# Another order for the sample rows' attention in a two-layer decoder step: page scores first, root transposes among the last keys, the block mask added by GpSimd

## The chip, the cores and the metric

The kernel runs on one core of one Trainium2 chip. The metric is the time of one execution on the device, in microseconds, and lower is better. The core has five engines with queues of their own: TensorE (PE; its weight loads stand as PEld), VectorE (DVE), ScalarE (ACT), GpSimd (POOL) and SyncE (SP, which here only starts transfers). Each engine works through its instructions in the order in which they are written, and waits at semaphores for the others.

## The reference, cut to what matters

One step of a decoder with two layers. 256 prompt rows and 8 x 4 sample rows go through the same weights. The second layer's mixer is sparse attention. The change lies in the part of it for the sample rows: for each of 8 sequences, 4 new rows with 16 heads look at 1024 past keys (16 blocks of 64, of which one in the middle is dropped: top 16 of 17), at the last 512 keys of a window, and at compressed keys.

```python
kb = to_blocks(rmsnorm(sel_full[:, :, 0], kn_g))            # 1024 past keys in blocks of 64, and the new ones
o_sel = selected_branch(q, kb, vb, idx, valid, q_pos, table)
...
    logits = jnp.einsum('btgpd,bngd->...', qg, kg) * SCALE  # sel and window branch alike
    p = masked_softmax(logits + bias, mask, axis=-1)        # the mask holds the unselected blocks
    o = jnp.einsum('...', p, v)
o = gates[:, :, 0] * o_cmp + gates[:, :, 1] * o_sel + gates[:, :, 2] * o_win
return o.reshape(B, T, C_HEADS * HEAD_DIM) @ w_out, ...
```

## The kernel before, in words

The whole step is one program. Activations lie transposed (features on partitions, 256 + 32 rows along the free axis), and each projection goes over units of 256 weight columns: SyncE loads a unit, ScalarE rounds it to its upper part (`wH`), VectorE forms the rest (`wL`), and TensorE multiplies both with the upper and lower part of the activations (`hH`, `hL`). Some 90% of the run is such units.

The sample attention stands between the prompt rows' attention and the output projection (`out_stage`), and nothing else runs on TensorE in that time. The 8 sequences go in 4 pairs, i = 0 to 3. For a pair, 128 partitions hold 2 sequences x 4 groups x 4 rows x 4 heads, and the tile `S` holds their scores: columns 0 to 1023 the pages (selected keys), 1024 to 1055 new keys, 1056 to 1567 the window (local keys), 1568 to 1599 new keys again. The steps of one pair, and who does them:

- **Keys.** The pair's keys come in three sets, c = 0 and 1 (pages) and c = 2 (window). For each set TensorE makes 16 transposes in four lots (`turn_keys`, L2218), into PSUM banks 4 and 5 in turn; ScalarE copies each lot to `KT` (`take_keys`, L1013); TensorE then scores the set into bank c (`score_keys`, L2230). Because there are two banks, lot m + 2 waits for the copy of lot m (`s_taken`). The same two banks serve all other transposes, and `turn_slot` gives each its place in the turn.
- **Norms of the keys.** ScalarE squares six pieces of 1024 (`square_keys`, L1025) into two buffers, VectorE sums each (`sum_squares_of`, L1644); piece n waits for the sum of piece n - 2. Then `variance` (VectorE, L1650), `roots` (ScalarE: a table load, the square root, a table load back, L1036 and L1037), `invert_roots` (VectorE, L1657), `turn_roots` (TensorE, L2239), `take_roots` (ScalarE, L1031), and `spread_roots` (TensorE, L2258), three times four matmuls that spread the factors over the key columns.
- **Softmax.** ScalarE copies the page scores from PSUM to `S` (`keep_scores`, L1046), VectorE the window scores (L1680). VectorE multiplies each of three sets by its factors (`normalise`, L1665), adds the bias (window L1688, pages L1698), adds the mask of the dropped block to the pages (L1702), and takes maxima (window L1691 and L1694, pages L1703 and L1704). ScalarE takes the exponentials (`exps_of`, L1052).
- **Weighing.** TensorE transposes the weights in four lots (`turn_weights`, L2269 and L2272: k = 0 window, 1 and 2 pages, 3 new keys), ScalarE copies them (`take_weights`, L1059 and L1061), TensorE multiplies with the values (`weigh_pages`, L2287, `weigh_new`, L2296). VectorE combines the branches (`gather`, L1718 to L1720), TensorE transposes the result (`turn_output`, L2315), VectorE places it in `zT` (`place_output`, L1730).

Pair i's softmax runs beside pair i + 1's keys; the order in which the pieces of the two stand in each engine's queue is written out by hand at the end of each engine's part. The keys and values of a sequence come by nine transfers for keys and nine for values (`sequence`, L454 to L457), issued by SyncE (even sequences) and GpSimd (odd ones), the keys for pair i + 2 once pair i's are used up, the values once pair i's weighing is over (`s_pv`). After pair 3, ScalarE splits two units of the output weights (`split_out`, L1066), then makes `hH` from `zT` in two halves over all 288 rows (L1113), VectorE makes the two units' `wL` (`lower_out`, L1737) and then `hL` in two halves (L1760), and TensorE begins the output projection (L1834).

Of the kernel before, what the change touches and what calls it, by code (L numbers as in the profile page):

```python
# [122 lines left out]
def emit(nc, a, out):  # L123

    with ExitStack() as ctx:
# [78 lines left out]
        kvs = sb("kvs", [NS, 12 * P], where=spot)  # L204
        KC = sb("KC", [P, NB, 2, 64], where=spot)
# [76 lines left out]
        assert spot[0] <= raw_at  # L282
        spot = [base + 12 * T * 4]
# [66 lines left out]
        bt_summed, bt_act, bt_dve = sem("bt_summed"), sem("bt_act"), sem("bt_dve")  # L350

# [77 lines left out]
        def turn_slot(kind, i, k=0):  # L429

            if i == 0 and kind in ("keys", "roots"):
                return k if kind == "keys" else 13
            if kind == "compressed":
                return 12
            if kind == "weights":
                at_ = (4, 9, 10, 11)[k]
            else:
                i, at_ = i - 1, 16 if kind == "roots" else k + (0, 1, 4)[k // 4]
            return 14 + 17 * i + (at_ if i < 3 else k)

        MULT = (1, 2, 0)
# [142 lines left out]
        def _(pool):  # L584
# [10 lines left out]
            def odd():  # L595
# [89 lines left out]
                for kv in range(2):  # L685
                    sequence(pool, 3, kv)
# [67 lines left out]
        def _(act):  # L754
# [115 lines left out]
            def odd():  # L870
# [134 lines left out]

                def take_keys(i, c):

                    for j in range(4):
                        m = turn_slot("keys", i, 4 * c + j)
                        act.wait_ge(s_turned, m + 1)  # L1010
                        if j == 0 and 3 * i + c >= 2:
                            act.wait_ge(s_scored, 3 * i + c - 1)
                        nc.scalar.activation(KT[(3 * i + c) % 2][:, j, :], ps[:, 4 + m % 2, :], ACT.Copy).then_inc(s_taken, 1)  # L1013
# [25 lines left out]
                def keep_scores(i):  # L1039

                    act.wait_ge(s_scored, 3 * i + 2)
                    if i > 0:
                        act.wait_ge(s_turned, turn_slot("weights", i - 1, 3) + 1)
                    else:
                        act.wait_ge(s_summed, 6)
                    nc.scalar.activation(S[:, 0:PAST], ps[:, 0:2, :].rearrange("p b n -> p (b n)"), ACT.Copy).then_inc(s_kept, 1)  # L1046

                def exps_of(i, k):

                    c0, c1 = ((1056, 1600), (0, 1056))[k]  # L1050
                    act.wait_ge(s_max, 2 * i + k + 1)
# [27 lines left out]
                roots(0)  # L1079
# [3 lines left out]
                nc.scalar.activation(PTc[:, :, :], ps[0:NCMP_S, 4 + m % 2, :].rearrange("p (i q) -> p i q", i=4), ACT.Copy).then_inc(s_taken, 1)  # L1083
                take_roots(0)
                keep_scores(0)
                for i in range(4):
                    if i < 3:
                        square_keys(i + 1, 0)
                        square_keys(i + 1, 1)
                        take_keys(i + 1, 0)  # L1090
                    exps_of(i, 0)
                    if i < 3:
                        square_keys(i + 1, 2)
                        square_keys(i + 1, 3)
                    take_weights(i, 0)
                    if i < 3:
                        take_keys(i + 1, 1)
                    exps_of(i, 1)
                    if i < 3:
                        square_keys(i + 1, 4)  # L1100
                        square_keys(i + 1, 5)
                    for k in range(1, 4):
                        take_weights(i, k)
                    if i < 3:
                        roots(i + 1)
                        take_keys(i + 1, 2)
                        keep_scores(i + 1)
                        take_roots(i + 1)
# [3 lines left out]
                for h in range(2):  # L1112
                    nc.scalar.activation(hH[:, 4 * h:4 * h + 4, :], zT[:, 4 * h:4 * h + 4, :], ACT.Copy).then_inc(ohi_done, 1)  # L1113
# [42 lines left out]
        def _(dve):  # L1156
# [228 lines left out]
            def odd():  # L1385
# [201 lines left out]
                def compressed_branch():  # L1587
# [27 lines left out]
                    sum_squares_of(0, 2)  # L1615
                    sum_squares_of(0, 3)
# [12 lines left out]
                    sum_squares_of(0, 4)  # L1629
                    sum_squares_of(0, 5)  # L1630
# [27 lines left out]

                def normalise(i, c):
# [13 lines left out]
                def softmax(i):  # L1673
# [5 lines left out]
                    dve.wait_ge(s_scored, 3 * i + 3)  # L1679
                    kept = mark(nc.vector.tensor_copy(S[:, 1056:1568], ps[:, 2, :]))  # L1680
                    new_keys(i, 0)
                    new_keys(i, 1)
                    dve.wait_ge(own, kept)
                    normalise(i, 2)
                    if i < 3:
                        sum_squares_of(i + 1, 0)
                    dve.wait_ge(s_mult, 3 * i + 1)
                    biased_ = mark(nc.vector.tensor_tensor(S[:, 1056:1568], S[:, 1056:1568], biasw[:, :], ALU.add))  # L1688
                    normalise(i, 0)
                    dve.wait_ge(own, biased_)  # L1690
# [781 lines left out]
```

## Time and profile before

| | us |
|---|---|
| median of 3 runs | 1770.28 (1765.61 to 1770.8) |
| the profiled execution | 1766.63 |
| its span, first to last instruction | 1764.9 |
| sample attention, TensorE's first score (1372.1) to the first matmul of the output projection (1497.4) | 125.3 |
| mean granted TensorE clock, share of full speed | 0.944 |

TensorE is busy 1591.1 us of the span (90%), VectorE 823.3 (47%), ScalarE 701.9 (40%) and GpSimd 201.7 (11%). A line of a timeline gives the start, how long the piece lasted (several like instructions may be merged, and xN is then their count), the engine, the line of the kernel, the operation with what it wrote and read, and in brackets how long the engine had been idle and what ended that. TensorE's matmuls are written x8 where the program has four: an fp32 product is made in two passes.

### The profile page before, as it was taken

To read this page: it belongs to the slowest core of one execution; us is meant where nothing else is said; L and a number is where in the kernel's file an instruction comes from. 1 tells how busy PE (TensorE), PEld (TensorE's weight loads), DVE (VectorE), ACT (ScalarE), POOL (GpSimd) and SP (SyncE) were. 2 spreads that over 40 slices of the span, in tenths; PEclk is the share of its full clock that TensorE was granted. 3 is DMA by queue.
4 is the path that set the end of the run, shared out by engine and by line. 5 is a ranking of instruction groups with operands and counts; after the bars stand their busy time and mean duration, and the time that the engine had idled before them with its cause. 6 is when DMAs were issued, how large, how long until landed. Compare 5 with 4: busy or idle time off the path is not lost.

```text
span 1764.9 us, 31479 instructions
## 1 busy us (share of the span) xinstructions
PE 1591.1 (90%) x11896; PEld 1438.8 (82%) x11896; DVE 823.3 (47%) x1191; ACT 701.9 (40%) x866; POOL 201.7 (11%) x323
## 2 busy tenths in 40 slices
PE   4799999898789999889999799899988675899997
PEld 2499998796789998779999698888866453899996
DVE  0344443677354443354444432344337765544442
ACT  1333333441343333243333323466446774333332
POOL 6000000193020000000000000222230330000000
PEclk9699999999889999989999789899989998999999
DMA  9667668542167668756755453243562563255442
GB/s 266 212 225 227 223 225 267 168 143 85 50 207 226 224 219 264 231 191 214 222 177 166 151 166 95 79 111 100 181 224 88 158 199 113 72 167 166 154 161 93
DMA packets 269003, 304.77 MB, mean 173 GB/s; under 512 B 9945, under 2 KB 257857, under 8 KB 268792
## 3 DMA queue, kind: packets, MB, share of 16 engines
q1 hardware_dynamic: 260304, 274.96, 49.2%
q0 software_dynamic: 8624, 28.77, 4.9%
q8 instruction: 51, 0.84, 0.2%
q14 instruction: 24, 0.20, 0.0%
HBM read 300.51 MB, written 11.92 MB: 177 GB/s over the span
## 4 chain that ended last, share of the span: by engine, by line
PE 77%; DVE 9%; DMA 7%; ACT 5%; issue 2%; SPq 0%; DVEq 0%; POOL 0%; ACTq 0%; POOLq 0%
PE ps L1834 12%; PE ps L1835 11%; PE ps L1838 11%; PE ps L2050 7%; PE ps L1816 7%; PE ps L1817 6%; PE ps L1818 6%; PE ps L1848 4%; DMA raw<-in_ffn_w_dram 3%; DMA ada<-in_ada_w_dram 2%; PE ps L2034 2%; PE ps L1863 1%; ACT wH L759 1%; DVE wL L1182 1%; PE ps L2147 1%
## 5 line engine op out<-in xcount | busy, mean ns | idle before, releaser
L1182 DVE TENSOR_TENSOR wL<-raw,wH 128x2048 fp32r<-128x2048 f32 (+2 forms) x176 | 365.7, 2078 | 423.1 <-ACT wH L759 423.0
L759 ACT ACTIVATE wH<-raw 128x2048 fp32r<-128x2048 f32 (+2 forms) x176 | 306.1, 1739 | 631.2 <-PE ps L1838 297.1
L1834 PE MATMUL ps<-hL,wH 128*128 128x288 f32 x1008 | 278.9, 304 | 17.1 <-DVE hL L1376 9.2
L1835 PE MATMUL ps<-hH,wH 128*128 128x288 f32 x1008 | 274.2, 298 | 0.0
L1816 PE MATMUL ps<-hH,wL 128*128 128x288 f32 x816 | 250.3, 307 | 12.7 <-DVE hL L1239 12.7
L1818 PE MATMUL ps<-hH,wH 128*128 128x288 f32 x816 | 246.2, 302 | 0.0
L1817 PE MATMUL ps<-hL,wH 128*128 128x288 f32 x816 | 246.1, 302 | 0.0
L1834 PEld LDWEIGHTS ps<-hL,wH 128*128 128x128 f32 x1008 | 192.0, 191 | 31.7 <-issue 13.6
L1834 PE MATMUL ps<-hidL,wH 128*128 128x288 f32 x704 | 194.4, 303 | 0.9 <-ACT wH L759 0.9
L1835 PEld LDWEIGHTS ps<-hH,wH 128*128 128x128 f32 x1008 | 191.9, 190 | 0.2
L1835 PE MATMUL ps<-hidH,wH 128*128 128x288 f32 x704 | 190.1, 296 | 0.0
L1816 PEld LDWEIGHTS ps<-hH,wL 128*128 128x128 f32 x816 | 159.2, 195 | 16.1 <-issue 16.1
L1817 PEld LDWEIGHTS ps<-hL,wH 128*128 128x128 f32 x816 | 159.1, 195 | 0.0
L1818 PEld LDWEIGHTS ps<-hH,wH 128*128 128x128 f32 x816 | 158.7, 194 | 0.0
L1838 PE MATMUL ps<-hH,wL 128*128 128x288 f32 x1008 | 144.0, 295 | 0.0
L1834 PEld LDWEIGHTS ps<-hidL,wH 128*128 128x128 f32 x704 | 132.4, 188 | 8.9 <-issue 8.4
L1838 PEld LDWEIGHTS ps<-hH,wL 128*128 128x128 f32 x1008 | 137.2, 188 | 0.0
L1835 PEld LDWEIGHTS ps<-hidH,wH 128*128 128x128 f32 x704 | 132.4, 188 | 0.5
L2050 PE MATMUL ps<-XT,w1c 128*128 128x252 f32 (+1 forms) x576 | 125.4, 379 | 0.9 <-DVE XT L1417 0.9
L2050 PEld LDWEIGHTS ps<-XT,w1c 128*128 128x128 f32 x576 | 109.5, 202 | 14.4 <-DVE XT L1417 1.1
L1838 PE MATMUL ps<-hidH,wL 128*128 128x288 f32 x704 | 103.9, 295 | 0.0
L1848 PE MATMUL ps<-ada,cT 128*32 128x256 f32 x1152 | 88.9, 432 | 15.2 <-DMA ada<-in_ada_w_dram 14.8
(380 smaller groups left out, 1913.2 us busy)
## 6 DMA issues: line engine op xcount, KB each, us to landing
raw<-in_ffn_w_dram SPq DMA_DIRECT2D x88, 1024.0 KB, 5.2
ada<-in_ada_w_dram SPq DMA_DIRECT2D x72, 1024.0 KB, 5.2
raw<-in_ffn_w_dram SPq DMA_DIRECT2D x32, 768.0 KB, 4.7
raw<-in_ffn_w_dram SPq DMA_DIRECT2D x32, 640.0 KB, 5.0
craw<-in_cache_cmp_kv_dram SPq DMA_DIRECT2D x64, 256.0 KB, 3.6
raw<-in_nsa_w_in_dram SPq DMA_DIRECT2D x10, 1024.0 KB, 5.3
raw<-in_even_w_in_dram SPq DMA_DIRECT2D x8, 1024.0 KB, 5.4
kvp<-in_cache_sel_kv_dram POOLq DMA_DIRECT2D x64, 128.0 KB, 3.4
```

The costliest lines, as they stand in the source:

```text
L759: nc.scalar.activation(wH[parity][:, 0:k * UW], raw[parity][:, 0:k * UW], ACT.Copy).then_inc(hi_done, 1)
L1182: nc.vector.tensor_tensor(wL[parity][:, 0:k * UW], raw[parity][:, 0:k * UW], wH[parity][:, 0:k * UW].bitcast(F32), ALU.subtract).then_inc( ...
L1816: nc.tensor.matmul(o, l_, rhsH, start=first, stop=False)
L1817: nc.tensor.matmul(o, h, rhsL, start=False, stop=False)
L1818: return nc.tensor.matmul(o, h, rhsH, start=False, stop=last)
L1834: nc.tensor.matmul(ps[:, banks + t, 0:T], wH[parity][:, c:c + P], L[:, k, :], start=first and k == k0, stop=False)
L1835: nc.tensor.matmul(ps[:, banks + t, 0:T], wH[parity][:, c:c + P], H[:, k, :], start=False, stop=False)
L1838: mm = nc.tensor.matmul(ps[:, banks + t, 0:T], wL[parity][:, c:c + P], H[:, k, :], start=False, stop=last and k == k1 - 1)
L1848: mm = nc.tensor.matmul(ps[32 * j:32 * j + 32, 6, 0:UW], cT[:, k, :], ada[ada_slot[third, u]][:, k, :], start=(i == 0), stop=(i == 1), ski ...
L1863: mm = nc.tensor.matmul(ps[:, SUM_BANK, 0:T], ones[:, :], tmp[:, c, :], start=(c == 0), stop=(c == KD - 1))
L2034: mm = nc.tensor.transpose(ps[:, n, P * g:P * g + P], cre[:, n, g, :, :].rearrange("p s d -> p (s d)"), ident)
L2050: mm = nc.tensor.matmul(ps[:, 4, 0:4 * n], w1c[:, v, c, :], pairs[:, :, c % 8, c // 8:c // 8 + n], start=(c == 0), stop=(c == 15))
```

## The change

In the sample attention the same values are computed, in another order and partly on other engines:

- **Page scores first.** VectorE's softmax of a pair begins with the new keys and the two page sets, and comes to the window set after them. `MULT` is now (0, 1, 2), `exps_of(i, 1)` (pages) stands before `exps_of(i, 0)` (window), and the weights of the pages are transposed and weighed first.
- **Roots among the last keys.** TensorE turns the roots of pair i + 1 after the first lot of its window keys, and the first two spreads stand between the later lots; before, they came after the score of that set. ScalarE copies the roots after the first of the four lots.
- **The mask goes to GpSimd.** A new tile `biasm` (1024 columns, in the place of `KC`) gets bias + mask from GpSimd (`mask_bias`), once for each pair, and VectorE adds `biasm` in one instruction; its own mask addition (L1702) is gone. The four instructions, and a copy of the first and last block ahead of them, stand between GpSimd's transfers: `mask_bias(0)` after the keys of sequence 3 and before its values, `mask_bias(1)` and `(2)` between keys and values of later sequences, `mask_bias(3)` at the end.
- **`keep_scores` goes from ScalarE to VectorE.**
- **For pair 0** all six sums and the variance stand before the choice of the dropped block on VectorE, and the table load with the root stands after the window keys' copies on ScalarE.
- **End of the stage.** The 256 prompt columns of `hH` and `hL` are made in pair 3's softmax (ScalarE ahead of its first exponential, VectorE behind its second maximum). After pair 3 only the 32 sample columns are left, and the two `wL` of `lower_out` stand behind `hL`.

```diff
-        MULT = (1, 2, 0)
+        MULT = (0, 1, 2)
...
+                def mask_bias(i):
+                    if i > 0:
+                        pool.wait_ge(s_max, 2 * i - 1)
+                    mask = E4[:, 2, 14 * i:14 * i + 14].rearrange("p (j n) -> p j n", n=1).to_broadcast([P, 14, 64])
+                    pool.tensor_tensor(biasm[:, 64:960].rearrange("p (j k) -> p j k", k=64), bias[:, 64:960].rearrange("p (j k) -> p j k", k=64),
+                                       mask, ALU.add).then_inc(laid, 1)
...
                 for i in range(2):
                     keys_read(pool, i)
                     sequence(pool, 5 + 2 * i, 0)
+                    mask_bias(i + 1)
                     pool.wait_ge(s_pv, 2 * i + 1)
                     sequence(pool, 5 + 2 * i, 1)
+                mask_bias(3)
...
+                def keep_scores(i):
+                    dve.wait_ge(s_scored, 3 * i + 2)
...
+                    nc.vector.tensor_copy(S[:, 0:PAST], ps[:, 0:2, :].rearrange("p b n -> p (b n)")).then_inc(s_kept, 1)
...
-                for u in range(2):
-                    lower_out(u)
-                for h in range(2):
-                    dve.wait_ge(ohi_done, h + 1)
-                    nc.vector.tensor_tensor(hL[:, 4 * h:4 * h + 4, :], ...).then_inc(o_split, 1)
+                lower_output(2)
+                for u in range(2):
+                    lower_out(u)
...
-                pe.wait_ge(o_split, 2)
+                pe.wait_ge(o_split, 3)
```

How the order moves, at three places. The names: `KT` the turned keys, `sqt` squares of keys, `PTs` turned weights, `kss` sums and roots, `smallS` maxima.

ScalarE, from the first page keys of pair 2 to the last weights of pair 1, before and then now:

```order
L1013 ACTIVATE KT_162<-ps 128x512 x4
L1052 ACTIVATE S,smallS<-S,smallS 128x544
L1025 ACTIVATE sqt_175<-kvp_132 128x1024
L1025 ACTIVATE sqt_176<-kvp_133 128x1024
L1059 ACTIVATE PTs<-ps 128x512
L1013 ACTIVATE KT_163<-ps 128x512 x4
L1052 ACTIVATE S,smallS<-S,smallS 128x1056
L1025 ACTIVATE sqt_175<-kvw_134 128x1024
L1025 ACTIVATE sqt_176<-kvw_135 128x1024
L1059 ACTIVATE PTs<-ps 128x512 x2
L1061 ACTIVATE PTs<-ps 32x256
```

```order
L1030 ACTIVATE KT_162<-ps 128x512 x4
L1065 ACTIVATE S,smallS<-S,smallS 128x1056
L1047 ACTIVATE sqt_176<-kvp_132 128x1024
L1072 ACTIVATE PTs<-ps 128x512 x2
L1047 ACTIVATE sqt_177<-kvp_133 128x1024
L1065 ACTIVATE S,smallS<-S,smallS 128x544
L1047 ACTIVATE sqt_176<-kvw_134 128x1024
L1047 ACTIVATE sqt_177<-kvw_135 128x1024
L1030 ACTIVATE KT_163<-ps 128x512 x4
L1072 ACTIVATE PTs<-ps 128x512
L1074 ACTIVATE PTs<-ps 32x256
```

The pages' exponential (1056 columns) has moved up and the window's (544) down, and the four copies of the second page keys now stand behind all six squares.

VectorE, the softmax of a pair from its first multiplication by the factors to its second maximum, before and then now:

```order
L1665 TENSOR_TENSOR S<-S,ps 128x512
L1644 TENSOR_REDUCE kss_168<-sqt_175 128x4x4
L1688 TENSOR_TENSOR S<-S,biasw 128x512
L1665 TENSOR_TENSOR S<-S,ps 128x512
L1691 TENSOR_REDUCE smallS<-S 128x1
L1665 TENSOR_TENSOR S<-S,ps 128x512
L1694 TENSOR_SCALAR smallS<-smallS 128x1
L1644 TENSOR_REDUCE kss_168<-sqt_176 128x4x4
L1698 TENSOR_TENSOR S<-S,bias 128x1024
L1702 TENSOR_TENSOR S<-S,E_170 128x896
L1703 TENSOR_REDUCE smallS<-S 128x1
L1704 TENSOR_SCALAR smallS<-smallS 128x1
```

```order
L1690 TENSOR_TENSOR S<-S,ps 128x512 x2
L1710 TENSOR_TENSOR S<-S,biasm 128x1024
L1711 TENSOR_REDUCE smallS<-S 128x1
L1712 TENSOR_SCALAR smallS<-smallS 128x1
L1660 TENSOR_REDUCE kss_169<-sqt_176 128x4x4
L1660 TENSOR_REDUCE kss_169<-sqt_177 128x4x4
L1717 COPY S<-ps 128x512
L1690 TENSOR_TENSOR S<-S,ps 128x512
L1720 TENSOR_TENSOR S<-S,biasw 128x512
L1721 TENSOR_REDUCE smallS<-S 128x1
L1722 TENSOR_SCALAR smallS<-smallS 128x1
```

The pages' maximum now comes ahead of the window's copy from PSUM, and two sums of squares stand between them.

ScalarE at the end of the stage, from the exponentials of pair 3 to the output projection, before and then now (`hH` the upper part of the attention's output):

```order
L1052 ACTIVATE S,smallS<-S,smallS 128x544
L1059 ACTIVATE PTs<-ps 128x512
L1052 ACTIVATE S,smallS<-S,smallS 128x1056
L1059 ACTIVATE PTs<-ps 128x512 x2
L1061 ACTIVATE PTs<-ps 32x256
L1066 ACTIVATE wH_67<-rawX_136 128x2048
L1066 ACTIVATE wH_68<-rawX_137 128x2048
L1113 ACTIVATE hH<-zT 128x1152 x2
```

```order
L1120 ACTIVATE hH<-zT 128x4x256 x2
L1065 ACTIVATE S,smallS<-S,smallS 128x1056
L1072 ACTIVATE PTs<-ps 128x512 x2
L1065 ACTIVATE S,smallS<-S,smallS 128x544
L1072 ACTIVATE PTs<-ps 128x512
L1074 ACTIVATE PTs<-ps 32x256
L1079 ACTIVATE wH_67<-rawX_136 128x2048
L1079 ACTIVATE wH_68<-rawX_137 128x2048
L1130 ACTIVATE hH<-zT 128x8x32
```

Of `hH` only 32 columns for each of 8 feature blocks are left behind the last weights; the two halves of 256 columns stand ahead of the first exponential.

## Rows read from the trace of the kernel before

**Rows 1.** Busy time by stretch: us, then each engine, granted clock, DMA share, GB/s

```profile
1420.10:1445.10 25.00, 18.32 (x225) 12.73 (x225) 17.72 (x30) 20.06 (x32) 9.78 (x19) 1.00 0.79 253
1470.10:1497.40 27.30, 10.82 (x152) 8.52 (x151) 17.82 (x30) 9.99 (x12) 0.00 (x0) 0.77 0.36 120
```

**Rows 2.** Timeline: pair 0's first factors, then pair 0's last weights to pair 1's

```profile
1394.63 1.16 PE L2258 MATMUL ps<-rT,spread 96*128 96x128 f32 x8
...
1411.14 0.37 ACT L1061 ACTIVATE PTs<-ps 32x256 f32<-32x256 f32 x1
...
1413.13 1.28 ACT L1037 ACT_TABLE_LOAD   x1
...
1420.10 2.02 PE L2258 MATMUL ps<-rT,spread 96*128 96x128 f32 x16
...
1426.05 0.15 DVE L1694 TENSOR_SCALAR smallS<-smallS 128x1 f32<-128x1 f32 x1
...
1430.91 0.15 DVE L1704 TENSOR_SCALAR smallS<-smallS 128x1 f32<-128x1 f32 x1
...
1436.15 0.37 ACT L1061 ACTIVATE PTs<-ps 32x256 f32<-32x256 f32 x1
```

**Rows 3.** Groups of instructions on VectorE in the sample attention: count, busy us, mean ns

```profile
L1644 DVE TENSOR_REDUCE kss<-sqt 128x16 f32<-128x1024 f32 x18 | 21.3, 1213 | 1.8 <-ACT sqt L1025 1.8
L1665 DVE TENSOR_TENSOR S<-S,ps 128x512 f32<-128x512 f32 x12 | 8.2, 681 | 0.0
L1703 DVE TENSOR_REDUCE smallS<-S 128x1 f32<-128x1056 f32 x4 | 5.0, 1253 | 0.1
L1698 DVE TENSOR_TENSOR S<-S,bias 128x1024 f32<-128x1024 f32 x4 | 4.9, 1220 | 0.0
...
L1702 DVE TENSOR_TENSOR S<-S,E 128x896 f32<-128x896 f32 x4 | 4.4, 1092 | 0.1
...
L1691 DVE TENSOR_REDUCE smallS<-S 128x1 f32<-128x544 f32 x4 | 2.9, 716 | 0.0
```

**Rows 4.** The same view for ScalarE: copies of turned keys, squares

```profile
L1013 ACT ACTIVATE KT<-ps 128x512 f32<-128x512 f32 x48 | 26.7, 594 | 9.5 <-PE ps L2218 9.2
L1025 ACT ACTIVATE sqt<-kvp 128x1024 f32<-128x1024 f32 x12 | 11.9, 1044 | 0.0
```

**Rows 5.** Timeline of pair 3: weights transposed at the full and at half the clock

```profile
1476.24 0.63 PE L2269 MATMUL ps<-const,S 128*128 128x128 f32 x4 [2.42 <-ACT S L1052]
...
1476.91 0.60 ACT L1059 ACTIVATE PTs<-ps 128x512 f32<-128x512 f32 x1 [0.81 <-PE ps L2269]
...
1480.46 1.94 PE L2269 MATMUL ps<-const,S 128*128 128x128 f32 x8 [3.59 <-ACT S L1052]
...
1481.59 0.60 ACT L1059 ACTIVATE PTs<-ps 128x512 f32<-128x512 f32 x1 [1.26 <-PE ps L2269]
```

**Rows 6.** Timeline: the end of the stage, up to the output projection

```profile
1487.28 0.42 PE L2296 MATMUL ps<-kvs,PTs 32*32 32x128 f32 x8
...
1490.34 4.49 DVE L1737 TENSOR_TENSOR wL<-rawX,wH 128x2048 fp32r<-128x2048 f32 x2
1490.34 2.22 ACT L1113 ACTIVATE hH<-zT 128x1152 fp32r<-128x1152 f32 x2 [3.42 <-DVE zT L1730]
...
1494.75 2.62 DVE L1760 TENSOR_TENSOR hL<-zT,hH 128x1152 fp32r<-128x1152 f32 x2
1497.42 0.29 PEld L1834 LDWEIGHTS ps<-hL,wH 128*128 128x128 f32 x1 [8.12 <-DVE hL L1760]
```

**Rows 7.** GpSimd's work of its own, groups over the whole run

```profile
L732 POOL TENSOR_SCALAR diag<-const,vecC 128x128 f32<-128x128 f32 x62 | 60.6, 995 | 3.4 <-PE ps L1924 3.3
L638 POOL COPY cre<-craw 128x512 f32<-128x512 f32 x64 | 38.1, 625 | 121.5 <-PE ps L2034 99.9 <-DMA craw<-in_cache_cmp_kv_dram 21.7
```

**Rows 8.** Timeline: GpSimd issues the last key transfer of sequence 5

```profile
1403.12 0.76 POOL L457 DMA_DIRECT2D kvw<-in_state_win_kv_dram  x1
```

**Rows 9.** DMA issues in the sample attention: KB each, median us from issue to landing

```profile
kvw<-in_state_win_kv_dram POOLq DMA_DIRECT2D x6, 512.0 KB, 5.8
```

More of the change, by code:

```diff
@@ L282, in emit @@
         assert spot[0] <= raw_at
+        biasm = sb("biasm", [P, PAST], where=[KC_at])
         spot = [base + 12 * T * 4]
@@ L682, in odd @@
                     sequence(pool, 1, kv)
+                def mask_bias(i):
[4 more added lines that the diff above has]
+                                       mask, ALU.add).then_inc(laid, 1)
                 pool.wait_ge(o_placed, 8)
                 pool.dma_start(spread[:, :, :], a["gcon"][0:96, G_SPREAD:G_SPREAD + 12 * P].rearrange("p (n q) -> p n q", q=P)).then_inc(late_landed, 16)
-                for kv in range(2):
-                    sequence(pool, 3, kv)
+                sequence(pool, 3, 0)
+                pool.wait_ge(s_small, 1)
+                pool.wait_ge(s_cmp, 3)
+                pool.tensor_copy(biasm[:, :].rearrange("p (j k) -> p j k", k=64)[:, 0:16:15, :],
+                                 bias[:, 0:PAST].rearrange("p (j k) -> p j k", k=64)[:, 0:16:15, :]).then_inc(laid, 1)
+                mask_bias(0)
+                sequence(pool, 3, 1)
                 for i in range(2):
@@ L1614, in compressed_branch @@
                     nc.vector.tensor_tensor(E, E, Sc4[:, :, 7:63].rearrange("p i (j k) -> p i j k", k=4)[:, :, :, 0], ALU.add).then_inc(s_cmp, 1)
-                    sum_squares_of(0, 2)
-                    sum_squares_of(0, 3)
+                    for n in range(2, 6):
+                        sum_squares_of(0, n)
+                    variance(0)
                     dve.wait_ge(s_small, 2)
@@ L1752, in odd @@
                         variance(i + 1)
+                        keep_scores(i + 1)
                         invert_roots(i + 1)
@@ L2290, in weigh_new @@
                 def weigh_new(i, br):
+                    pe.wait_ge(s_taken, turn_slot("weights", i, 3) + 1)
                     for j in range(4):
@@ L2317, in odd @@
                 score_small()
-                for half in range(2):
-                    turn_keys(0, 0, half)
+                turn_keys(0, 0)
                 score_keys(0, 0)
-                for half in range(2):
-                    turn_keys(0, 1, half)
+                turn_keys(0, 1)
                 pe.wait_ge(s_cmp, 2)
@@ L2325, in odd @@
                 score_keys(0, 1)
-                for half in range(2):
-                    turn_keys(0, 2, half)
+                turn_keys(0, 2)
                 m = turn_slot("compressed", 0)
@@ L2342, in odd @@
                     if i < 3:
-                        turn_keys(i + 1, 0, 1)
+                        turn_key(i + 1, 0, 2)
+                        turn_key(i + 1, 0, 3)
                         score_keys(i + 1, 0)
-                    turn_weights(i, 0)
+                    turn_weights(i, 1)
+                    turn_weights(i, 2)
                     if i < 3:
-                        for half in range(2):
-                            turn_keys(i + 1, 1, half)
+                        turn_key(i + 1, 1, 0)
+                        turn_key(i + 1, 1, 1)
@@ L2349, in odd @@
+                    weigh_pages(i, 1)
+                    if i < 3:
+                        turn_key(i + 1, 1, 2)
+                        turn_key(i + 1, 1, 3)
+                    else:
+                        turn_weights(i, 0)
+                    weigh_pages(i, 2)
+                    if i < 3:
                         score_keys(i + 1, 1)
-                    for k in range(1, 4):
-                        turn_weights(i, k)
+                        turn_weights(i, 0)
+                    turn_weights(i, 3)
```

194 lines of the change are left out of this document (100 added, 94 removed).

## The prediction, made before the changed kernel ran

> **What bounds the kernel now.** I read the page first: TensorE is busy for 90% of the span, but the change lies in a stage of 125.3 us in which it is not the bound. So the busy times by stretch come next. In a middle pair's 25.0 us TensorE, VectorE and ScalarE are busy 18.3, 17.7 and 20.1 us [rows 1]: none is full, and each waits for the others in turn. The last 27.3 us hold only 10.8 us of TensorE, at 0.77 of its clock [rows 1]. The stage is thus a chain, and the timeline shows which. I set zero where ScalarE has copied a pair's last weights: 1411.5 for pair 0, 1436.5 for pair 1 (start plus length of L1061), 1461.5 for pair 2 by the same period of 25.0 us [rows 2]. From zero the chain runs over ScalarE's root with its two table loads (to 2.9), the window keys' turning, copying and score, and only then root transposes and spreads (8.6), the window's maximum (1426.05 + 0.15, so 14.7), the pages' maximum (19.5), and from there over exponential, squares and copies back to zero [rows 2].
>
> **The steady pairs, step by step.** All times are us from zero. Root: ScalarE as before until 2.9; VectorE's reciprocal is ready at 2.4. TensorE, whose weighing for the pair before now ends at 1.8, transposes the roots at 2.4. ScalarE first copies one lot of keys (2.9 to 3.5) and then the roots (3.65). TensorE has then in its queue: a lot of keys (0.47) from 3.5, the output's transpose (0.1), a lot (0.47), spread 0 (0.95), a lot, spread 1. The 2.02 us of two spreads [rows 2] give 1.0 for one with its end, so spread 1 is over at 7.0; it was 10.6.
> - VectorE multiplies both page sets (the second from 7.1, 0.68), adds bias and mask in one (1.22), takes the maximum (1.25) and negates (0.15) [rows 2, 3]: first maximum at 10.5. The removed mask addition would have been 1.09 more here [rows 3].
> - Then two sums of 1.13 each with overlap (1.21 alone), the window copy (0.69, like a multiplication), multiplication 0.68, bias 0.69, maximum 0.72, negation 0.15, each some 0.03 behind the other [rows 3]: 2.2 + 3.1, second maximum at 15.7. It was 19.5, so 3.8 us are won here. What is late next?
> - ScalarE. Its order now has squares 5 and 6 ahead of the second page keys' copies. Square 5 waits for the third sum, square 6 for the fourth: these are VectorE's next two, done at 16.9 and 18.0. Square 6 is done at 18.0 + 1.04 = 19.05 [rows 4]. Four copies of 0.59 [rows 4] in two banks, each pair of banks filled again by TensorE (0.67 from transpose to copy [rows 5]): last copy done at 21.4.
> - TensorE: score 1.0, window weights transposed from 22.5, 0.67 to the copy [rows 5], which with the last one (0.37 [rows 2]) ends at **24.1**: the new period, against 25.0. Of 3.8 us won, 2.9 are given back in this wait on squares and copies.
>
> `keep_scores` costs VectorE some 1.2 us (1024 columns, as L1698 [rows 3]), between 22.6 and 23.8, while ScalarE copies weights: covered, and the reciprocal is due at 25.7. Without that cover it would cost its 1.2 a pair.
>
> **The start, pair 0.** Before, the first spread begins at 1394.63 [rows 2]. Now ScalarE goes on with window keys at 1384.2 instead of waiting for the root's input; last key copy 1386.6, compressed weights copied 1387.5, root 2.9 us, its transpose at 1390.0, spreads from 1390.7 and (behind `compressed_output`) 1391.7 to 1392.7. Steps as above: first maximum at 1396.15, which is 10.5 after a zero at 1385.65, so pair 0's weights end at 1385.65 + 24.1 = 1409.75 against 1411.5: **1.75 us** won.
>
> **GpSimd.** No row shows its addition of two inputs. Below, its copy of 512 columns takes 0.625 us, so 896 take 1.1; above, its 128-column multiplication takes 0.995, which by columns gives 7.0 for 896 [rows 7]. I take 2.2, the copy's rate twice for two inputs, since the shape is nearest to the copy's. The Trainium skill, "GPSIMD Engine Reference", section 3.1, gives 4497 ns for such an addition of 2048 columns; an estimate from that page is 2.0 us, and its section 8 warns that two-input VectorE work and GpSimd share ports. No run here shows either, and the sum does not use them. With 2.2: the choice of the block is known at 1387.6 (it stands behind all sums now), `mask_bias(0)` ends near 1390.1 and is wanted at 1393.5. Behind it are queued the values of sequence 3 (wanted only at 1425) and the keys of sequence 5: their last issue moves from 1403.12 [rows 8] to about 1409.8, with 5.8 to landing [rows 9] 1415.6, wanted by square 2 of pair 2 at 1409.75 + 7.7 = 1417.4. Covered by 1.8 us. Later: values of sequence 5 from 1411.6, keys of 7 and their mask by 1435, wanted at 1441.6. SyncE's queue has no new entry.
>
> **The end.** From zero of pair 2 to the output projection's first weight load it is 1497.42 - 1461.5 = 35.9 us [rows 2, 6]. Now: first maximum at 10.5; ScalarE makes the prompt columns of `hH` from 8.1 (score 3 done) to 10.1, two of about 1.0 (2.22 for two of 1152 [rows 6]): idle time there, so no cost; were it busy, 2 us. No sums follow, so the second maximum is at 13.45. Exponential 0.95, transposes 0.67 to the copy, `weigh_pages(3, 2)`, last lot's copy 16.8, new and window values to 18.5. Combining 1.4, transpose 0.3, placing 0.8: 21.1. Before, from the weighing's end (1487.28 + 0.42) to placing done (1490.3) 2.6 as well, but then 7.1 us more: `wL` 4.49 and `hL` 2.62 on VectorE [rows 6]. Now ScalarE rounds 8 x 32 columns (1.11 x 256/1152 plus 0.2: 0.45), VectorE subtracts (0.35): **21.95**. So 13.95 us won: 6.2 behind the placing, and 7.7 ahead of it. `wL` is hidden: it is wanted after 32 matmuls of the first unit (over 4 us), and done 2.3 after their start.
>
> **The sum.** 1.75 + 2 x 0.9 + 13.95 = 17.5 us. I take 1.5 off for TensorE's clock (below), so 16: the profiled execution's 1766.63 becomes 1750.6. The median of the runs shown is 3.65 above it, so I predict 1770.28 - 16 = **1754**.
>
> **Rivals.**
> - *The clock falls in the new hole* (18%). After weighing page set 1 (16.2) TensorE now has nothing until 19.6, since its next transposes wait for those copies: 3.4 us idle in every middle pair. In pair 3 an idle time of 2.42 left it at the full 2.4 GHz (4 transposes 0.63), one of 3.59 behind little work was followed by half of it, 1.2 GHz (8 in 1.94) [rows 5]. At half clock what follows the hole costs: turn to copy 1.13 instead of 0.67 twice (0.9), weighing 0.7, score 1.0: 2.6 a pair, 7.8 in three, total gain 9.7, so 1760.5. For it: 3.4 is near 3.59. Against: here the work around the hole is denser. The forecast takes a fifth of it (1.5). The Trainium skill, "TensorE: Matmul & The Clock Gate", section "HAM oscillation", says that a kernel whose TensorE waits between bursts loses its clock in every one; by that rule the time would be this rival's.
> - *More is won* (10%). The output projection starts at half clock before, at the cost of some 2 us, and the tail has 0.77 [rows 1]. The last idle times now are 1.5 and 1.7 instead of 7.9; if the clock holds, 19.5 to 20 won: 1750.5.
> - *Only the end pays* (7%). If the order costs each pair what it wins and pair 0 starts no sooner: 14, less clock: 1757.
> - *Slower, by GpSimd* (3%, and 2% for other causes). If its addition takes X, pair 0 waits X - 5.6, and each of pairs 1 and 2 about X - 4 (behind its own mask and sequence 5's and 7's keys). At the upper end, 7.0, that is 1.4 + 3 + 3: a gain of 10, 1760. From X = 10.5 the 17.5 us are spent, at 12 it is 6.4 + 8 + 8 = 22: 1775.
>
> **How the numbers follow.** 60% for the forecast (1751 to 1757 by itself), 18% clock, 10% more, 7% end only, 5% slower or spent. A measurement of this kernel tells changes from 0.3% (5.3 us) on. Faster by more than that: the first four, less some weight for errors of my walk: 0.88. Within: 0.08; slower: 0.04. The range for 8 in 10 goes from the clock kept (1750, less 2 for runs at the lower level of 1765.6) to the clock rival with 1 more: 1748 to 1762.
>
> **What would show it.** Right: period of the last weights' copies near 24.1, squares 5 and 6 of a pair waiting for VectorE's sums, first maximum some 4 us sooner after zero, `hL` of 32 columns right behind the placing, stage 108 to 110 us long. Wrong: transposes of 0.95 instead of 0.55 behind the hole (clock); VectorE's addition of `biasm` waiting for GpSimd, or a square waiting for a key transfer (GpSimd's queue); a wait of TensorE for `wL` in the first output unit.

## The result, and the profile after

The changed kernel takes 1760.98 us, the median of 5 runs (1758.41 to 1761.82); the kernel before took 1770.28 (1765.19 to 1771.04) beside it. The ratio is 0.9954, 95% interval 0.9935 to 0.9972: faster, by 8 to 9 us, where 16 had been forecast. Five more rounds on another chip gave 0.9952 (0.9936 to 0.9969). The profiled execution took 1758.41 us with a span of 1756.4, against 1766.63 and 1764.9.

From TensorE's first score (1370.83) to the first matmul of the output projection (1487.65) the stage now takes 116.8 us instead of 125.3. With zero again where ScalarE has copied a pair's last weights (start plus length of L1074, which was L1061), it falls into these parts:

| us | before | predicted | after | with TensorE kept busy in the idle times (two runs, below) |
|---|---|---|---|---|
| first score to zero of pair 0 | 39.4 | 37.65 | 39.35 | 37.7 |
| zero of pair 0 to zero of pair 1 | 25.0 | 24.1 | 26.9 | 24.1 |
| pair 1 to pair 2 | 25.0 | 24.1 | 27.2 | 24.4 |
| zero of pair 2 to the output projection | 35.9 | 21.95 | 23.3 | 22.4 |
| sum | 125.3 | 107.8 | 116.8 | 108.6 |

The last column puts two runs together: the pairs are from the kernel with work in the three holes of pairs 0 to 2, the end from the one with work in pair 3, and 108.6 is no run's stage. So each middle pair has become slower than before, and the end alone pays for them. The busy times by stretch answer to [rows 1] (columns as there): a middle pair, the end, and a piece of the middle pair.

```profile
1410.18:1437.07 26.89, 20.74 (x226) 14.48 (x225) 18.22 (x30) 19.40 (x30) 11.84 (x19) 0.87 0.77 236
1464.31:1487.65 23.34, 15.60 (x225) 11.17 (x223) 14.76 (x33) 15.53 (x21) 0.00 (x0) 0.91 0.28 92
...
1429.81:1435.30 5.49, 5.49 (x49) 3.33 (x49) 1.11 (x2) 1.63 (x3) 4.07 (x5) 0.50 0.89 257
```

VectorE and ScalarE are as busy as in [rows 1] to within 0.7 us. TensorE has a like number of matmuls (226 for 225) and is busy 2.4 us more, at a granted clock of 0.87 where it had 1.00, and 0.50 (1.2 GHz) in the piece of 5.5 us. The timeline of pair 1 shows what comes ahead of that piece; it answers to [rows 2] and [rows 5].

```profile
1409.82 0.36 ACT L1074 ACTIVATE PTs<-ps 32x256 f32<-32x256 f32 x1
...
1420.54 0.15 DVE L1712 TENSOR_SCALAR smallS<-smallS 128x1 f32<-128x1 f32 x1
...
1425.77 0.15 DVE L1722 TENSOR_SCALAR smallS<-smallS 128x1 f32<-128x1 f32 x1
...
1427.09 2.18 ACT L1047 ACTIVATE sqt<-kvw 128x1024 f32<-128x1024 f32 x2 [0.28 <-DVE kss L1660]
...
1429.18 1.07 ACT L1030 ACTIVATE KT<-ps 128x512 f32<-128x512 f32 x2
1429.81 1.97 PE L2243 MATMUL ps<-const,kvp 128*128 128x128 f32 x8 [3.38 <-ACT KT L1030]
...
1431.71 1.93 PE L2317 MATMUL ps<-kvp,PTs 128*32 128x128 f32 x32
...
1433.42 1.93 PE L2260 MATMUL ps<-KT,QB 128*32 128x512 f32 x8
...
1435.28 0.90 PE L2299 MATMUL ps<-const,S 128*128 128x128 f32 x4
...
1436.71 0.36 ACT L1074 ACTIVATE PTs<-ps 32x256 f32<-32x256 f32 x1
```

Read it from zero at 1410.18. The pages' maximum is found at 10.5, the window's at 15.7, the window squares wait for VectorE's sums (0.28 <-DVE kss), and the second page keys' first copy starts at 19.0: the walk of the prediction to a tenth. TensorE has waited for that copy, and has idled for 3.38 us when it goes on at 1429.81. What it does next takes 1.97, 1.93 and 1.93 us instead of 1.14, 1.08 and 1.07 at the full clock. The last stretch of the stage reads so:

```profile
1476.27 1.46 PE L2299 MATMUL ps<-const,S 128*128 128x128 f32 x8 [2.89 <-ACT S L1065]
...
1477.66 1.94 PE L2317 MATMUL ps<-kvp,PTs 128*32 128x128 f32 x32
...
1485.58 0.30 PE L2346 MATMUL ps<-const,O 128*64 128x128 f32 x1 [1.51 <-DVE O L1738]
1485.91 0.78 DVE L1748 COPY zT<-ps 64x32 f32<-64x32 f32 x4 [0.39 <-PE ps L2346]
...
1487.17 0.43 DVE L1761 TENSOR_TENSOR hL<-zT,hH 128x256 fp32r<-128x256 f32 x1 [0.48 <-ACT hH L1130]
1487.51 4.49 DVE L1755 TENSOR_TENSOR wL<-rawX,wH 128x2048 fp32r<-128x2048 f32 x2
1487.65 0.61 PE L1859 MATMUL ps<-hL,wH 128*128 128x288 f32 x1 [1.77 <-DVE hL L1761]
...
1488.30 0.44 PE L1859 MATMUL ps<-hL,wH 128*128 128x288 f32 x1
...
1494.78 2.30 PE L1863 MATMUL ps<-hH,wL 128*128 128x288 f32 x16
```

`hL` of 32 columns stands right behind the placing, and nothing waits for `wL`. But the first 32 output matmuls take 7.1 us (1487.65 to 1494.78); they took 6.35 before.

### The profile page after: what moved, and what is told of

The parts are those of the page before. It is cut to its first block, busy times and chain, and to the rows that moved or that the text cites. A ratio compares the mean times of both kernels' runs of the same rounds, so it can differ in the third digit from the quotient of the medians.

```text
span 1756.4 us, 31479 instructions
## 1 busy us (share of the span) xinstructions
PE 1596.7 (91%) x11896; PEld 1442.7 (82%) x11896; DVE 825.3 (47%) x1192; ACT 699.1 (40%) x863; POOL 210.0 (12%) x328
## 4 chain that ended last, share of the span: by engine, by line
PE 78%; DVE 8%; DMA 7%; ACT 4%; issue 1%; SPq 0%; DVEq 0%; POOL 0%; ACTq 0%; POOLq 0%
PE ps L1859 12%; PE ps L1860 11%; PE ps L1863 11%; PE ps L2075 7%; PE ps L1841 6%; PE ps L1843 6%; PE ps L1842 6%; DMA raw<-in_ffn_w_dram 4%; PE ps L1873 4%; PE ps L2059 2%; DMA ada<-in_ada_w_dram 2%; ACT wH L777 1%; DVE wL L1199 1%; PE ps L2172 1%; PE ps L1888 1%
```

## The experiments

Each kernel is told as a difference from the one named. Times are medians with the ratio to the kernel before on the same chip; periods and stage lengths come from the traces. Medians of one kernel differ by 0.1 to 0.2% between chips and rounds, and the stage begins anywhere from 1365.3 to 1372.4 us in the traces, for reasons ahead of it. The stage lengths of the three kernels that were traced twice agree within 0.2 us (the changed kernel's 116.8 twice), so mechanisms are read from the traces.

**Work in TensorE's hole.** The changed kernel with 24 transposes of a constant, which nobody reads, where TensorE waits for ScalarE's copies; what the kernel returns does not depend on them.

```diff
+                def fill(n):
+
+                    for _ in range(n):
+                        nc.tensor.transpose(ps[:, 1, 0:P], const[:, C_ANTI:C_ANTI + P], ident)
...
                     weigh_pages(i, 1)
                     if i < 3:
+                        fill(24)
                         turn_key(i + 1, 1, 2)
```

> The changed kernel with 24 dummy transposes (128 x 128, the reversal matrix into PSUM bank 1, which the next score overwrites) put into TensorE's idle time behind the weighing of page set 1, for pairs 0 to 2. Nothing else is changed; the added results are used by nobody. Theory (the clock): in the changed kernel TensorE idles 4.2, 3.4 and 3.7 us there and works at half its clock behind it; kept busy, it keeps 2.4 GHz. The two periods between last weights go from 26.9 and 27.2 us to 24.3, the four transposes behind the place from 0.95 a lot to 0.55, and the time falls by three times 2.6 to 1753. Rival (the period is long because ScalarE's copies come late, and the clock only shows it): the periods stay at 26.9, the time at 1761, or is 1 us more by the added work.

Measured: 1751.98 us, ratio 0.9922 (0.9891 to 0.9953). Stage 109.7 us, periods 24.1 and 24.4. A middle pair's busy times, then its timeline:

```profile
1408.30:1432.42 24.12, 20.74 (x250) 15.40 (x249) 18.22 (x30) 19.29 (x30) 12.01 (x20) 1.00 0.78 248
```

```profile
1424.48 2.84 PE L2351 MATMUL ps<-const 128*128 128x128 f32 x24
...
1427.93 1.14 PE L2243 MATMUL ps<-const,kvp 128*128 128x128 f32 x8 [0.61 <-ACT KT L1030]
...
1429.01 1.08 PE L2317 MATMUL ps<-kvp,PTs 128*32 128x128 f32 x32
1429.90 1.04 PE L2260 MATMUL ps<-KT,QB 128*32 128x512 f32 x8
```

The wait for the copies is as long as before, yet TensorE works through most of it, keeps 1.00 of its clock, and the same three pieces take 1.14, 1.08 and 1.04 us. The period is the 24.1 of the walk. Adding work of no use took 7.1 us out of the stage.

**The same work where there is no hole.** A control: the kernel before, with 8 unread transposes behind the window's weights and 8 ahead of the new keys' weights, both in idle times of 1.22 us.

```diff
                     turn_weights(i, 0)
                     if i < 3:
+                        fill(8)
...
                     for k in range(1, 4):
+                        if i < 3 and k == 3:
+                            fill(8)
                         turn_weights(i, k)
```

> A control: the kernel before the change, whose middle pairs keep the full clock, with twice 8 unread transposes a pair in two idle times of TensorE of 1.22 us each (behind the window's weights, and ahead of the new keys' weights). Output unchanged. Clock theory: with nothing to hold there is nothing to win, periods of 25.0 us and the time of before (ratio 1.00, stage 125.3 us). Rival (unread transposes help by some other way than the clock, by waking TensorE or by placing its reads): the periods become shorter than 25.0.

Measured: 1764.69 us, ratio 0.9992 (0.9973 to 1.001), stage 125.4 us. A middle pair:

```profile
1407.48:1432.50 25.02, 20.07 (x243) 14.49 (x241) 17.73 (x31) 20.07 (x31) 8.18 (x15) 1.00 0.53 169
```

25.0 as before. Here unread work brought something only where a hole had cost the clock.

**Take the hole away.** The changed kernel, with ScalarE's four copies of the second page keys ahead of the window's exponential and of the last square, as soon as their banks are full.

```diff
                     square_keys(i + 1, 3)
+                    take_key(i + 1, 1, 0)
+                    take_key(i + 1, 1, 1)
                     exps_of(i, 0)
                     square_keys(i + 1, 4)
+                    take_key(i + 1, 1, 2)
+                    take_key(i + 1, 1, 3)
                     square_keys(i + 1, 5)
-                    take_keys(i + 1, 1)
```

> The changed kernel with another order on ScalarE alone: the first two copies of page set 1's turned keys stand ahead of the window's exponential, the last two between squares 5 and 6, the weights' copies behind square 6. Theory (the hole is made by those copies standing behind both squares, which wait for VectorE's sums): TensorE gets its next lots at 16 instead of 19.6 us after zero, idles nowhere longer than some 2 us, keeps its clock, and the period falls to 22.4 us; time 1748. If only the clock were to blame and the copies' place not, the clock is kept and the period is 24.1: 1753. If the hole only moves (TensorE now waits behind lot 4 for the window's weights, which stand behind square 6) and the clock falls there, 26: 1759.

Measured: 1745.55 us, ratio 0.9892 (0.9864 to 0.9919). Stage 102.8 us, periods 21.7 and 21.8, 0.7 us shorter than expected. ScalarE's timeline:

```profile
1415.59 1.10 ACT L1030 ACTIVATE KT<-ps 128x512 f32<-128x512 f32 x2
1416.55 0.78 ACT L1065 ACTIVATE S<-S,smallS 128x544 f32<-128x544 f32 x1
...
1417.28 1.09 ACT L1047 ACTIVATE sqt<-kvw 128x1024 f32<-128x1024 f32 x1
1418.22 1.12 ACT L1030 ACTIVATE KT<-ps 128x512 f32<-128x512 f32 x2
1419.18 1.11 ACT L1047 ACTIVATE sqt<-kvw 128x1024 f32<-128x1024 f32 x1
```

No bracket stands in these rows: the copies fill the time in which ScalarE waited for a maximum or a sum. TensorE's hole is gone (its longest idle time in the middle pairs is 0.98 us, and 1.50 in pair 0), and 2.4 us a pair come off beside: most of the 2.9 us that the walk had given back in this very wait. The end takes 24.3 us, 1.0 more than in the changed kernel: behind the same idle time of 2.89 us in pair 3 the first eight transposes take 1.94 us instead of 1.46.

**One part of the change at a time.** The kernel before, with the new end of the stage only (`hH` and `hL` in prompt and sample columns, `wL` behind `hL`):

```diff
+                    if i == 3:
+                        act.wait_ge(s_scored, 12)
+                        for h in range(2):
+                            nc.scalar.activation(hH[:, 4 * h:4 * h + 4, 0:NP_], ...)
...
+                lower_output(2)
                 for u in range(2):
                     lower_out(u)
-                for h in range(2):
-                    ... hL[:, 4 * h:4 * h + 4, :] ...
```

> The kernel before with only the end of the stage changed: prompt columns of hH and hL made in pair 3's softmax, the two lower parts of the weights behind hL. Theory: behind the placing of pair 3 some 0.9 to 1.3 us are left of 7.1, so 6 us are won, minus up to 1 us for a longer stretch at half clock in the output projection: 1764 to 1765. Rival 1: all of the change's gain is this one, 1761. Rival 2: the lower parts of the weights, now behind, hold up the output projection: 1768 to 1770.

Measured: 1760.99 us, ratio 0.9979 (0.996 to 0.9997). Periods 25.0, stage 119.3 us, so 6.0 less. From the end of the placing to the output projection it takes 0.97 us instead of 7.12, so 6.15 less, where the walk had 6.2. The median is the one of the rival, that this part is all of the change's gain; but it comes from another chip than the changed kernel's 1760.98. The ratios (0.9979 against 0.9954) and the stages (119.3 against 116.8) leave 2.5 us of the stage to the rest of the change.

The changed kernel with the mask added by VectorE again and nothing of it on GpSimd, and the same with the 24 transposes:

```diff
-                    link(nc.vector.tensor_tensor(S[:, 0:PAST], S[:, 0:PAST], biasm[:, :], ALU.add))
+                    link(nc.vector.tensor_tensor(S[:, 0:PAST], S[:, 0:PAST], bias[:, 0:PAST], ALU.add))
+                    link(nc.vector.tensor_tensor(dropped, dropped, mask, ALU.add))
```

> The changed kernel with the mask added by VectorE again, as its own instruction behind the bias, and nothing of it on GpSimd. Theory (pages' maximum stands at the head of the chain): the first maximum is 1.1 us later in each of four pairs, 4.4 us more in all: 1765. Rival (the mask's 1.1 us is covered, since the exponential waits for ScalarE's key copies, which end 0.9 us behind the maximum): 0 to 1 us more, 1761 to 1762.

> The changed kernel with the mask added by VectorE again (median 1760.40, periods 26.7 and 26.8) and the 24 unread transposes in each middle hole. Theory: the mask's 1.09 us do lie on the path (the first maximum is found at 11.6 instead of 10.5), and without the fill they were hidden only because the clock happened to come back 1.2 us sooner behind the hole; with the clock held, periods of 25.2 us against 24.1 to 24.4 of the fill alone, four times 1.09 = 4.4 us more than 1751.98: 1756. Rival (the mask is covered by squares and copies): periods of 24.1 and 1752.

Measured without the fill: 1760.4 us, ratio 0.9959 (0.9943 to 0.9976), periods 26.7 and 26.8, as if the mask cost nothing. With it: 1757.06, ratio 0.9941 (0.9916 to 0.9967), periods 25.2 and 25.2 against 24.1 and 24.4. So the mask costs 1.1 us in the first of them, the whole addition, and 0.8 in the second, where the 24.4 hold 0.3 us that GpSimd's addition causes (last section). The first maximum is found at 11.6 instead of 10.5. Two timeline rows without the fill say why the first comparison misleads, then a middle pair's busy times with it:

```profile
1434.57 1.66 PE L2239 MATMUL ps<-const,kvp 128*128 128x128 f32 x8 [4.18 <-ACT KT L1023]
...
1437.88 1.27 PE L2256 MATMUL ps<-KT,QB 128*32 128x512 f32 x8
```

```profile
1409.66:1434.84 25.18, 20.74 (x250) 15.40 (x249) 19.31 (x31) 19.40 (x30) 10.09 (x18) 1.00 0.74 228
```

The hole had grown from 3.38 to 4.18 us, but the full clock came back sooner behind it (1.27 for the score instead of 1.93), and the one hid the other. Only in the middle pairs, though: the stage of this trace is 121.3 us long, 4.5 more than the changed kernel's, with 3.0 more in pair 0, where the half clock came among the spreads (last section), and 2.1 more at the end. The median of its ten runs (1755.19 to 1764.24) does not show them, and the traced one took 1763.24.

The changed kernel with the 24 transposes, and the roots of pairs 1 to 3 turned, copied and spread behind the window keys' score, as before the change:

```diff
                     if i < 3:
-                        turn_roots(i + 1)
                         turn_key(i + 1, 2, 1)
...
                         turn_key(i + 1, 2, 2)
-                        spread_roots(i + 1, 0)
                         turn_key(i + 1, 2, 3)
-                        spread_roots(i + 1, 1)
                         score_keys(i + 1, 2)
+                        turn_roots(i + 1)
+                        spread_roots(i + 1, 0)
+                        spread_roots(i + 1, 1)
```

> The changed kernel with the 24 unread transposes in each middle hole (which gave 1751.98 and periods of 24.1 and 24.4), and the roots of pairs 1 to 3 turned, copied and spread behind the window keys' score, as before the change; pages still come first and GpSimd still makes the mask. My walk: first maximum 3.6 us later after zero (14.1 instead of 10.5), and everything behind it too, so periods of 27.7 us, three times 3.6 = 11 us more: 1763. Rival (the squares and copies of ScalarE, not the first maximum, set the period, so part of the 3.6 is covered): periods of 25 to 26, 1755 to 1758.

Measured: 1758.55 us, ratio 0.9945 (0.992 to 0.997), periods 26.5, between the walk's and the rival's:

```profile
1408.84:1435.30 26.46, 20.98 (x250) 15.35 (x249) 20.16 (x30) 19.36 (x31) 12.97 (x20) 1.00 0.80 250
```

The first maximum comes at 12.85 instead of 10.5, so 2.35 later, and the period is 2.35 longer: every part of the delay is paid, as the walk says. But the delay is 2.35 and not 3.6. The expectation had given all 3.6 us to the roots' place. The other 1.3 belong to the pages' weighing, as the timelines of the kernel before and, below it, of this one say:

```profile
1416.15 1.95 PE L2287 MATMUL ps<-kvp,PTs 128*32 128x128 f32 x64
...
1418.38 1.07 PE L2230 MATMUL ps<-KT,QB 128*32 128x512 f32 x8
...
1419.73 0.27 ACT L1031 ACTIVATE rT<-ps 96x128 f32<-96x128 f32 x1 [1.95 <-PE ps L2239]
```

```profile
1414.42 1.07 PE L2258 MATMUL ps<-KT,QB 128*32 128x512 f32 x8 [0.74 <-ACT KT L1030]
```

Before, the window keys' score began 6.9 us after zero, although their last copy ended at 5.35, since TensorE first weighed both page sets (the 64 matmuls). With the pages weighed earlier it begins at 5.6. `keep_scores`, then on ScalarE, held up nothing here: ScalarE idled for 1.95 us behind it, until TensorE had turned the roots.

**The end of the stage.** The changed kernel with unread transposes in pair 3 alone: 20 behind the third spread, 9 ahead of the output's transpose, 11 ahead of the output projection.

```diff
                     spread_roots(i, 2)
+                    if i == 3:
+                        fill(20)
...
+                    if i == 3:
+                        fill(9)
                     turn_output(i)
+                    if i == 3:
+                        fill(11)
```

> The changed kernel, and in pair 3 alone TensorE gets work that nobody reads: 20 transposes of a constant behind the third spread (2.4 us, in an idle time of 2.89), 9 ahead of the output's transpose (in 1.51), 11 ahead of the output projection (in 1.77). Everything else and the output are unchanged. Clock theory: the two page weight lots go to 0.55 each instead of 1.46 for the first eight transposes, the pages' weighing to 1.08 instead of 1.94, and the first output matmuls to a pitch of 0.13 instead of 0.24 us; from the last zero to the output projection about 22 us instead of 23.3, and some 2.6 us less behind its start: 3.5 to 4 us less than the changed kernel in all, about 1757. The pairs before keep their periods of 26.9 and 27.2. Rival (the 0.24 pitch at the start of the output projection has another cause, such as the wL made beside it or its weights' loads): the pitch stays at 0.24 and the time within 1 us of 1761.

> The changed kernel again, to stand beside the next two on one chip. Ratio 0.995 as measured first, stage 116.8 us.

> The changed kernel with the unread transposes in pair 3 alone, again: its trace showed 1.0 us less from the last zero to the output projection and 2.9 us less behind that start, but its time could not be told from the changed kernel's (0.9947, interval 0.9924 to 0.997). If what the trace shows is kept to the end, 3.9 us less than the changed kernel on the same chip (ratio 0.993). Rival (given back later, as the output projection then waits for its weights): no difference.

Measured: 1756.97 us, ratio 0.9947 (0.9924 to 0.997), and again, beside the changed kernel on one chip, 1755.11 with 0.9938 (0.9915 to 0.996) against 1759.92 with 0.9952. The intervals overlap, so the times alone don't settle it; the traces do. Timeline of the first run:

```profile
1470.71 2.35 PE L2351 MATMUL ps<-const 128*128 128x128 f32 x20
1473.78 1.06 PE L2299 MATMUL ps<-const,S 128*128 128x128 f32 x8 [0.71 <-ACT S L1065]
...
1482.25 1.36 PE L2351 MATMUL ps<-const 128*128 128x128 f32 x11
1484.19 0.40 PE L1859 MATMUL ps<-hL,wH 128*128 128x288 f32 x1 [0.58 <-DVE hL L1761]
1484.43 0.29 PE L1860 MATMUL ps<-hH,wH 128*128 128x288 f32 x1
...
1488.58 1.61 PE L1863 MATMUL ps<-hH,wL 128*128 128x288 f32 x11
```

The end takes 22.4 us instead of 23.3, and the first 32 output matmuls 4.4 us instead of 7.1. From the projection's start to the end of the span it is 266.0 us instead of 268.75 in both runs, so that 2.7 us is not given back. In all 3.7 us.

**All together.** The early copies and the transposes in pair 3:

> The kernel with the second page keys' copies ahead of the window's exponential (median 1745.55), with the same 20 + 9 + 11 unread transposes in pair 3. It should show the periods of 21.7 us, and win in the tail what the fill wins in the changed kernel: 3.5 to 4 us, so 1742. If the clock at the start of the output projection is not what the tail loses, 1745.

> The kernel with the second page keys' copies ahead of the window's exponential and the unread transposes in pair 3, again, as the fastest so far: ratio 0.9875 as before, periods of 21.7 us.

Measured: 1744.41 us, ratio 0.9875 (0.9838 to 0.9913), and again 1741.89, ratio 0.9856 (0.9828 to 0.9883). Stage 101.0 and 100.9 us. A middle pair and the end, in the second run:

```profile
1407.41:1429.10 21.69, 18.06 (x226) 12.77 (x225) 18.45 (x31) 18.83 (x30) 11.87 (x20) 1.00 0.81 258
1450.91:1473.28 22.37, 18.68 (x265) 14.32 (x263) 15.74 (x34) 15.42 (x21) 0.00 (x0) 1.00 0.30 96
```

By the second run it beats both kernels: 1.4% below the kernel before, 1.0% below the changed one, on one chip.

## Why the prediction's direction was right and its size wrong

The direction and the range (1748 to 1762) held. The size did not: 16 us were forecast, 8 to 9 came. The time is that of the rival "the clock falls in the new hole", 1760.5 us, to which only 18% had been given.

- **The step that failed** is the weight of that rival. The prediction found the hole, its length (3.4 us; the traces have 4.18, 3.38 and 3.66 in pairs 0, 1 and 2) and its price (2.6 us a pair; the fill returns 2.8 in each of pairs 1 and 2, and 1.65 in pair 0), and then took a fifth of it, because "the work around the hole is denser" than in [rows 5]. [rows 1] do show denser work, but no row showed that such work keeps the clock through a hole of this length. In pair 1 no idle time of TensorE between zero and the hole is longer than 0.74 us, and it still falls to 0.50 of its clock. The rule of the Trainium skill that was weighed there ("TensorE: Matmul & The Clock Gate", section "HAM oscillation": waits between bursts lose the clock in every one) fits: all three holes are followed by half clock. In pair 0 it comes one piece later than in pairs 1 and 2 (the transposes behind the hole still take 1.14 us, the weighing then 1.94), which is why less is lost there.
- **The ledger.** Of the 17.5 us of the walk the stage won 8.5. The 9.0 that are missing lie in pair 0 (1.7), pair 1 (2.8), pair 2 (3.1) and the end (1.4). The clock has 8.3 of them (1.65 + 2.8 + 2.8 + 1.0) by the two fills. Of the rest, 0.3 in pair 2 is GpSimd's doing (last section), and 0.4 at the end are small misses that add up. With the fill of pair 3 the second maximum comes at 13.5 as predicted, but the last lot is copied at 16.95 (predicted 16.8), all values are weighed at 18.8 (18.5), `zT` is placed at 21.4 (21.1), and the projection starts 0.97 behind that (0.85). The 1.5 that were taken off for the clock should have been 8.3.
- **The steady pairs** were walked rightly: maxima at 10.5 and 15.7 as predicted, period 24.1 with the clock held. Of the 3.6 us by which the second spread ends sooner, 2.35 are the roots' new place and 1.3 the earlier weighing, which the prediction had too. And the 2.9 us "given back in this wait on squares and copies" were taken as a fact of the stage, though only the order made them: moving the four copies takes 2.4 us or more off each middle pair.
- **Pair 0** has its 1.75 us when the clock is held (37.7 against 39.4).
- **The end:** 6.15 measured behind the placing for 6.2, `wL` hidden as said. The rival "more is won" rested on a clock that holds through idle times of 1.5 and 1.7 us. They are 1.51 and 1.77 with one transpose between them, and the projection starts at half clock, for longer than before. That costs 0.8 us behind the stage (7.13 instead of 6.35 for the first 32 matmuls), for which the sum had no term. The price of the half clock there in the kernel before, put at some 2 us, is 6.35 - 4.39 = 1.96 over these matmuls.
- **GpSimd:** 1.70 us for its addition, where 2.2 was taken (bounds 1.1 to 7.0). The estimate from the Trainium skill, "GPSIMD Engine Reference", section 3.1, was 2.0. VectorE never waits for `biasm`, and the last key transfer of sequence 5 is issued at 1407.23, earlier than the 1409.8 of the walk. The mask's 1.1 us a pair are won, and on the path.

## What to carry to other kernels

Where an order is changed, list the idle times of TensorE that it makes, and price what follows each at half clock unless a row shows a like idle time that kept it; three holes of 3.4 to 4.2 us and one of 2.9 in the last pair took back 8 of the 17 us won here. An engine that is to wait for a maximum or a sum should first be given the copies that free TensorE's banks. When two versions are compared, compare them with the clock held as well, since a hole can hide what an edit costs.

## What the runs showed of the hardware that was not expected

**Shorter idle times also lose the clock.** Behind 2.42 us of idle time the clock was kept in [rows 5]. Behind 2.89 us (changed kernel, 1476.27) it is lost within the next piece, and it is kept behind the same wait when TensorE is idle for 0.71 us of it. Not all of it is explained: in the kernel with the mask on VectorE the two first spreads of pair 0 ran at half clock (3.76 us instead of 2.02), behind the same idle time of 0.47 us that cost the changed kernel nothing. And in the kernel with the mask on VectorE and the fill, half clock comes in pair 3 behind idle times of no more than 0.75 us (1463.57 and on; one of 1.41 stood 8 us ahead), so that its end takes 27.3 us instead of 23.5, where the mask explains 1.1. What tells these places apart is open; no run was made for it.

**GpSimd's addition holds up some of VectorE's instructions.** Timeline of the changed kernel (the addition of `biasw` in pair 1, then in pair 2 beside GpSimd), and below it of the kernel with the roots moved back:

```profile
1424.30 0.69 DVE L1720 TENSOR_TENSOR S<-S,biasw 128x512 f32<-128x512 f32 x1
...
1449.90 1.70 POOL L691 TENSOR_TENSOR biasm<-bias,E 128x896 f32<-128x896 f32 x1
...
1451.19 0.97 DVE L1720 TENSOR_TENSOR S<-S,biasw 128x512 f32<-128x512 f32 x1
```

```profile
1405.29 0.21 DVE L1664 TENSOR_SCALAR kss<-kss 128x96 f32<-128x96 f32 x1
...
1431.74 2.27 DVE L1664 TENSOR_SCALAR kss<-kss 128x96 f32<-128x96 f32 x1
1432.24 1.70 POOL L691 TENSOR_TENSOR biasm<-bias,E 128x896 f32<-128x896 f32 x1
```

The addition of two SBUF tiles takes 0.97 us instead of 0.69, and again 0.95 to 0.97 in pair 2 of seven other traces. A small in-place instruction takes 2.27 instead of 0.21: it ends at 1434.01, GpSimd's at 1433.94. This was seen once, and it is recorded as starting 0.5 us ahead of GpSimd's addition, so why it was held so early is open. Beside such GpSimd instructions VectorE's copies and multiplications from PSUM (0.68, 0.69), its sums (1.2 each) and its reciprocal (0.75) keep their times. The Trainium skill, "GPSIMD Engine Reference", section 8, warns of contention with VectorE instructions that read two SBUF inputs or run in a two-port mode. The prediction had set this aside as shown by no run; the trace now agrees for two SBUF inputs. Which mode the in-place instruction runs in, no run shows. It costs 0.3 us in this kernel, once; by the lower fence an estimate of what it could cost is up to 2 us (2.27 - 0.21) each time that a small instruction on the path is met so.
